# Differential attention with split scores, ScalarE taking over steps of VectorE, and new portions of the merge products (Trainium2, one core)

## The reference

```
q_d = dq.reshape(B, N, H_D, 2, DK_D)          # H_D = 4, DK_D = 64
k_d = dk.reshape(B, N, H_D, 2, DK_D)
v_d = dv.reshape(B, N, H_D, DV_D)             # DV_D = 128
if latent:
    q_d = _rope(q_d, cos_d, sin_d)
    k_all = concat([ctx[2], _rope(k_d, cos_d, sin_d)])   # 128 cached + 512
    v_all = concat([ctx[3], v_d])
p = softmax(q0 k0^T / 8) - lam * softmax(q1 k1^T / 8)
o_d = p @ v
o_d = _rms(o_d, diff_norm_g) * (1 - lam_init)
y = g_m * (o_m @ w_br_mlstm) + g_a * (o_a @ w_br_mla) + g_d * (o_d @ w_br_diff)
```

## Time and profile before

| what | value |
|---|---|
| three runs | 2631.68, 2633.82, 2633.03 us; median 2633.03 |
| the profiled execution | 2634.0 us, span 2632.2 us |
| PE busy | 2533.6 us (96%), 17328 products |
| PEld busy | 2367.1 us (90%) |
| DVE busy | 1250.5 us (48%), 1699 instructions |
| ACT busy | 750.8 us (29%), 1373 instructions |
| POOL busy | 1330.7 us (51%), 607 instructions |
| differential attention | 569 to 721 us in layer 0, 1863 to 2015 in layer 1 |
| dq/dk stage | ends at 541 us in layer 0, at 1824 in layer 1 |

### The profile page before, as it was taken

One profiled execution on the slowest core, in us unless ns is written; L12 is line 12 of the kernel. 1 busy time (PEld: TensorE's weight loads), 2 busy tenths in 40 slices (PEclk: granted clock), 3 DMA queues, 4 the chain that ended last, 5 costly groups with the idle time before them and its releaser, 6 DMA issues.

```text
span 2632.2 us, 41789 instructions
## 1 busy us (share of the span) xinstructions
PE 2533.6 (96%) x17328; PEld 2367.1 (90%) x17328; DVE 1250.5 (48%) x1699; ACT 750.8 (29%) x1373; POOL 1330.7 (51%) x607
## 2 busy tenths in 40 slices
PE   5999999999999999999989999999999999999997
PEld 3989986888899999999978899778888999999997
DVE  5443255866735423132554523659565363132235
ACT  3251355213322303021222513550334123112031
POOL 2535530453356666666654466106434666666664
PEclk8999999999999999999998999999999999999999
DMA  6202224531121222222211122342111222222221
GB/s 262 71 22 68 73 103 161 189 117 41 41 73 65 73 76 77 72 74 80 73 64 49 36 68 74 127 165 71 64 41 49 72 73 73 72 81 73 73 75 63
DMA packets 62556, 215.34 MB, mean 82 GB/s; under 512 B 6688, under 2 KB 11168, under 8 KB 62112
## 3 DMA queue, kind: packets, MB, share of 16 engines
q1 hardware_dynamic: 56448, 203.97, 22.7%
q10 hardware_dynamic: 5920, 8.70, 0.9%
HBM read 208.15 MB, written 4.49 MB: 81 GB/s over the span
## 4 chain that ended last, share of the span: by engine, by line
PE 84%; DVE 7%; issue 3%; ACT 2%; POOL 1%; DVEq 1%; DMA 1%; SPq 1%; POOLq 0%; ACTq 0%
PE big L517 21%; PE big L520 21%; PE big L521 21%; PE four L703 3%; PE big L774 3%; PE four L786 2%; PE four L599 2%; PE four L805 2%; PE big L543 1%; PE big L726 1%; PE big L546 1%; PE big L547 1%; PE four L746 1%; DVE prob_d L1651 1%; DVE prob_d L1649 1%
## 5 line engine op out<-in xcount | busy, mean ns | idle before, releaser
L481 POOL TENSOR_TENSOR w_hi<-raw,cst 128x1024 fp32r<-128x1024 f32 x288 | 552.8, 1919 | 1177.5 <-PE big L517 886.6
L517 PE MATMUL big<-act_hi,w_hi 128*128 128x320 f32 x2528 | 790.3, 313 | 6.6 <-issue 5.6
L520 PE MATMUL big<-act_lo,w_hi 128*128 128x320 f32 x2528 | 785.3, 311 | 0.0
L521 PE MATMUL big<-act_hi,w_lo 128*128 128x320 f32 x2528 | 785.1, 311 | 0.0
L484 POOL TENSOR_TENSOR w_lo<-raw,w_hi 128x1024 fp32r<-128x1024 f32 x288 | 742.7, 2579 | 41.0
L517 PEld LDWEIGHTS big<-act_hi,w_hi 128*128 128x128 f32 x2528 | 478.6, 189 | 16.0 <-issue 14.7
L520 PEld LDWEIGHTS big<-act_lo,w_hi 128*128 128x128 f32 x2528 | 478.6, 189 | 0.7
L521 PEld LDWEIGHTS big<-act_hi,w_lo 128*128 128x128 f32 x2528 | 478.3, 189 | 0.0
L517 PE MATMUL big<-u_hi,w_hi 128*128 128x320 f32 (+1 forms) x1024 | 319.0, 312 | 1.9 <-DVE u_lo L2071 1.9
L520 PE MATMUL big<-u_lo,w_hi 128*128 128x320 f32 (+1 forms) x1024 | 317.4, 310 | 0.0
L521 PE MATMUL big<-u_hi,w_lo 128*128 128x320 f32 (+1 forms) x1024 | 317.1, 310 | 0.0
(11 more groups left out here) (306 smaller groups left out, 3832.8 us busy)
## 6 DMA issues: line engine op xcount, KB each, us to landing
raw<-in_w SPq DMA_DIRECT2D x368, 512.0 KB, 3.4
first_mod<-in_first SPq DMA_DIRECT2D x16, 512.0 KB, 15.7
x<-in_x ACTq DMA_DIRECT2D x1, 2560.0 KB, 13.1
out_y<-x SPq DMA_DIRECT2D x8, 320.0 KB, 2.6
cst<-in_const ACTq DMA_DIRECT2D x1, 1664.0 KB, 7.8
small<-in_small ACTq DMA_DIRECT2D x2, 437.0 KB, 9.2
out_C<-c_new ACTq DMA_DIRECT2D x2, 258.0 KB
v_d<-in_past ACTq DMA_DIRECT2D x2, 256.0 KB, 2.9
```

The source lines that it names most:

```text
L481: nc.gpsimd.tensor_tensor(w_hi[:, to, :], raw[:, slot, :], ones[:, 0:1].to_broadcast([P, BLK]), ALU.mult)
L517: first = mm(ps, wh, ah, start=k == 0, stop=False)
L520: mm(ps, wh, al, start=False, stop=False)
L521: last = mm(ps, wl, ah, start=False, stop=k == nk - 1)
```

## The change

It has six parts. (1) The 42 portions of merge_a are cut anew: 21 pairs of slots, of each pair 5/14 in the even slot and 9/14 in the odd one. (2) q and k of the differential attention are split into rounded part and remainder: ACT makes kd_hi, qd_hi and qd_ctx_hi (`keys_hi`, `queries_hi`), DVE kd_lo and qd_lo (`keys_lo`, `queries_lo`), for head 0 ahead of the attention, for heads 1 to 3 in the middle of the head before; scores are three products each (q_hi k_hi, q_hi k_lo, q_lo k_hi). (3) In the dq/dk stage ACT makes the crossed copies of the 32-row groups and the copy of the context columns, out of the bank, and DVE keeps three operations. (4) DVE multiplies only the column of factors by neg_lam; ACT scales the second map by it (`scale_second`), and DVE adds. (5) ACT copies the outputs; turn waits for that only ahead of its fifth piece. ACT's order in a unit is new: outputs, exponential of map 0, copyT, exponential of map 1, gates, scaling, gates, parts of q and k. (6) split_y is spread: of k = 0 to 7, three at m = 5, one at m = 6 and four at m = 7, instead of six, one and one. The squares of heads move to the space of k_d and to i % 5 == 3.

```diff
-SLOTS = 2 * (5 * H_D + 1)
+SLOTS = 5 * H_D + 1
+SLOT_PARTS, SLOT_FIRST = 14, 5
-    return 4 * PAIR_PRODUCTS * slot // SLOTS
+    return 4 * PAIR_PRODUCTS * (SLOT_PARTS * (slot // 2) + SLOT_FIRST * (slot % 2)) // (SLOT_PARTS * SLOTS)
...
+        crossed = [rs, sq[:, 0, :]]
-        head_sq = [sq[:, 0, :], sq[:, 1, :], rs[:, :], prob_d[:, 0, :]]
+        head_sq = [k_d[:, 0, 0:T], k_d[:, 1, 0:T], k_d[:, 2, 0:T], prob_d[:, 0, :]]
...
+                    if t == 0:
+                        pe.wait_ge(qk_split, l * 8 + 2 * h + 2)
-                        for m, use in enumerate(uses):
-                            last = mm(ps[:, c, 0:w], q_d[r, h, q0:q1], k_d[r, h, k0 + c * w:k0 + c * w + w],
-                                      start=True, stop=True)
+                        for term, (q, kk) in enumerate(((q_hi, k_hi), (q_hi, k_lo), (q_lo, k_hi))):
+                            for m, use in enumerate(uses):
+                                r = slice(64 * m, 64 * m + 64)
+                                last = mm(ps[:, c, 0:w], q[r, :], kk[r, :], start=term == 0, stop=term == 2)
...
                 def turn(i):
-                    if i:
-                        pe.wait_ge(out_copied, l * 20 + i)
                     for c in range(1 if t == LATE else 5):
+                        if c == 4 and i:
+                            pe.wait_ge(out_copied, l * 20 + i)
...
+            def keys_hi(l, h):
+                f(kd_hi[:, h % 2, :], k_d[:, h, :], ACT.Copy).then_inc(qk_hi, 1)
+            def queries_hi(l, h):
+                f(qd_ctx_hi[:, h % 2, :], q_d[:, h, 0:CTX], ACT.Copy)
+                f(qd_hi[:, h % 2, :], q_d[:, h, CTX:T], ACT.Copy)
...
+                def scale_second(i):
+                    act.wait_ge(second_factor, l * 20 + i + 1)
+                    f(prob_d[:, c1, 0:w], prob_d[:, c1, 0:w], ACT.Copy, scale=row_sum[:, c1:c1 + 1]).then_inc(second_scaled, 1)
+                def outputs(i):
+                    act.wait_ge(o_ready, l * 60 + 40 + i + 1)
+                    f(q_d[:, h, q0:q1], out_d[i % 2], ACT.Copy).then_inc(out_copied, 1)
                 for i in range(-1, n):
+                    if i >= 1:
+                        outputs(i - 1)
                     if i + 1 < n:
-                        exps(i + 1)
+                        exps(i + 1, (0,))
+                    if i >= 0:
+                        copyT(i)
+                    if i + 1 < n:
+                        exps(i + 1, (1,))
                     if i >= 0:
                         half_gates(l, 2 * i + 2)
-                        copyT(i)
+                    if i + 1 < n:
+                        scale_second(i + 1)
                     half_gates(l, 2 * i + 3)
-                    if i > 5 and i % 5 == 1:
-                        head_square(l, (i - 6) // 5)
+                    if 0 <= i < 15 and i % 5 == 0:
+                        keys_hi(l, i // 5 + 1)
+                    if 0 <= i < 15 and i % 5 == 1:
+                        queries_hi(l, i // 5 + 1)
+                    if i > 5 and i % 5 == 3:
+                        head_square(l, (i - 8) // 5)
...
-                    f(two_parts(stage[:, m % 2, :]), halves(t), ACT.Copy, scale=DK_D ** -0.5 if m < 4 else 1.0)\
-                        .then_inc(free[b], 1)
+                    f(two_parts(stage[:, m % 2, :]), halves(t), ACT.Copy, scale=scale)
+                    for g in range(4):
+                        r, o = slice(32 * g, 32 * g + 32), slice(32 * (g ^ 1), 32 * (g ^ 1) + 32)
+                        f(two_parts(crossed[m % 2][o, :]), halves(t)[r], ACT.Copy, scale=scale)
+                    f(dst[:, 0:CTX], t[:, 0, 0:CTX], ACT.Copy, scale=scale).then_inc(free[b], 1)
...
-                    v.tensor_scalar(p1, p1, row_sum[:, c0 + 1:c0 + 2], neg_lam, ALU.mult, ALU.mult)
+                    v.tensor_scalar(row_sum[:, c0 + 1:c0 + 2], row_sum[:, c0 + 1:c0 + 2], neg_lam, None, ALU.mult)\
+                        .then_inc(second_factor, 1)
+                    dve.wait_ge(second_scaled, l * 20 + i + 1)
                     v.scalar_tensor_tensor(p0, p0, row_sum[:, c0:c0 + 1], p1, ALU.mult, ALU.add).then_inc(p_ready, 1)
...
+                    if 0 <= i < 15 and i % 5 == 1:
+                        keys_lo(l, i // 5 + 1)
+                    if 0 <= i < 15 and i % 5 == 2:
+                        queries_lo(l, i // 5 + 1)
...
-                    for g in range(4):
-                        v.tensor_tensor(t2[o, CTX:T], src[r, CTX:T], c_("sin_d", r), ALU.mult)
-                    v.tensor_copy(dst[:, 0:CTX], src[:, 0:CTX])
+                    v.tensor_tensor(t2[:, CTX:T], crossed[m % 2][:, CTX:T], c_("sin_d"), ALU.mult)
...
-                    for k in range(0, 6) if m == 5 else ([m] if m > 5 else []):
+                    for k in {5: (0, 1, 2), 6: (3,), 7: (4, 5, 6, 7)}.get(m, ()):
```

More of the change, by code:

```diff
@@ L289, in trunk @@
         tanh_d = [stage[:, 0, :], stage[:, 1, :], prob_d[:, 2, :], prob_d[:, 3, :]]
-        head_sq = [sq[:, 0, :], sq[:, 1, :], rs[:, :], prob_d[:, 0, :]]
+        head_sq = [k_d[:, 0, 0:T], k_d[:, 1, 0:T], k_d[:, 2, 0:T], prob_d[:, 0, :]]
+        kd_hi, kd_lo = at("kd_hi", [P, 2, TK], rs_at, f32r), at("kd_lo", [P, 4, TK], A0 + 10240, f32r)
+        qd_hi, qd_lo = at("qd_hi", [P, 2, LAT], A0 + 70656, f32r), at("qd_lo", [P, 4, T], A0, f32r)
+        qd_ctx_hi = at("qd_ctx_hi", [P, 2, CTX], rs_at + 6144, f32r)
         probT_d = at("probT_d", [P, 2, 5, P], A0 + 45056)
@@ L720, in scores @@
                         wait_free(pe, l, use)
+                    if t == 0:
+                        pe.wait_ge(qk_split, l * 8 + 2 * h + 2)
                     w = (k1 - k0) // (1 if t == LATE else 2)
+                    q_hi = qd_ctx_hi[:, h % 2, :] if t == LATE else qd_hi[:, h % 2, P * t:P * t + P]
+                    q_lo = qd_lo[:, h, q0:q1]
                     for c in range((k1 - k0) // w):
[L723 to L729 removed]
+                        z = slice(k0 + c * w, k0 + c * w + w)
+                        k_hi, k_lo = kd_hi[:, h % 2, z], kd_lo[:, h, z]
+                        for term, (q, kk) in enumerate(((q_hi, k_hi), (q_hi, k_lo), (q_lo, k_hi))):
+                            for m, use in enumerate(uses):
+                                ps, b, _ = buf(use)
+                                r = slice(64 * m, 64 * m + 64)
+                                last = mm(ps[:, c, 0:w], q[r, :], kk[r, :], start=term == 0, stop=term == 2)
+                                if term == 2 and c == (k1 - k0) // w - 1:
+                                    last.then_inc(ready[b], 1)
                 def turn(i):
@@ L1139, in attend_d, with exps @@
                 n = len(units)
-                def exps(i):
+                def exps(i, maps):
                     h, t = units[i]
@@ L1144, in exps @@
                         act.wait_ge(pT_ready, l * 60 + 40 + i - 1)
-                    for m in range(2):
+                    for m in maps:
                         ps, b, _ = buf(USE["da"][2 * i + m])
@@ L1624, in half_branches, with keys_lo, queries_lo @@
                     dve.drain()
+            def keys_lo(l, h):
+                dve.wait_ge(qk_hi, l * 8 + 2 * h + 1)
+                dve.wait_ge(dk_stored, l * 16 + 16)
+                v.tensor_tensor(kd_lo[:, h, :], k_d[:, h, :], kd_hi[:, h % 2, :].bitcast(f32), ALU.subtract)\
+                    .then_inc(qk_split, 1)
+            def queries_lo(l, h):
+                dve.wait_ge(qk_hi, l * 8 + 2 * h + 2)
+                v.tensor_tensor(qd_lo[:, h, 0:CTX], q_d[:, h, 0:CTX], qd_ctx_hi[:, h % 2, :].bitcast(f32), ALU.subtract)
+                v.tensor_tensor(qd_lo[:, h, CTX:T], q_d[:, h, CTX:T], qd_hi[:, h % 2, :].bitcast(f32), ALU.subtract)
+                dve.drain().then_inc(qk_split, 1)
             def attend_d(l):
@@ L2252, in _constants @@
         put("cos_" + name, np.tile(np.concatenate([c, c]), (P // dim, 1)))
-        sign = [z, -z] if name == "d" else [-z, z]
-        put("sin_" + name, np.tile(np.concatenate(sign), (P // dim, 1)))
+        put("sin_" + name, np.tile(np.concatenate([-z, z]), (P // dim, 1)))
     p, q = np.arange(P)[:, None], np.arange(P)[None, :]
```

36 lines of the change are left out of this document (21 added, 15 removed).

## The result

The changed kernel takes 2637.59 us in the median of 13 runs (2636.02 to 2641.67), the kernel before 2632.81 (2631.10 to 2634.53, 13 runs): the ratio is 1.0021, with a 95% interval of 1.0014 to 1.0028. It is slower by 4.8 us; forecast were 18.

The account below looks back on a forecast made before the run. PE was taken to bound the kernel, with 84% of the chain. Attention +13.2, rotation +4.9 and split_y 0 made +18.1 us on the profiled 2634.0, so 2651 against the median of the runs; the range was 2618 to 2674.

Parts of the forecast that it names:

- What bounds the kernel, and the excursions to DVE: Whole chain: PE holds 84%; in the attention, six excursions a layer to DVE are long when POOL splits a weight block.
- Scores as three products: Attention scores: a latent unit takes 1.08 us instead of 1.28, a context unit slightly more; -2.8 us a layer.
- Rival (c): Attention scores: weight loads of the pairs are not hidden, 1.74 us a unit, +10.5 a layer, 2672 us; chance 0.11.
- the floor of 1.28: Attention scores: by a Trainium skill rule, twelve loads of 0.107 us allow no gain, making the total 2657 us.
- The second map through ScalarE: Attention: copyT, scaling and hand-overs make each of six excursions 1.2 us longer, +7.2 us a layer.
- Rival (a): Attention: POOL does not hold the column product, so excursions come to -2.0 us a layer; about 2633 us, chance 0.22.
- Remainders of q and k: Attention: one head's three DVE operations stand on the path, +4.0 us a layer, between 0 and +8.
- Outputs: Attention: the output copy leaves DVE for ScalarE, -0.3 us in each of six excursions, -1.8 a layer.
- Portions: Attention, merge_a: the new cuts leave PE's work the same and move only cover; counted at nothing.
- Rotation of dq and dk: dq/dk stage: extra ScalarE copies cost 7.1 us in layer 0, layer 1 gains 2.25; net +4.9 us.
- split_y: Behind the gates: k = 7's remainder still sets the end of wout's first tile; 0, between -4.3 and +1.5 us a layer.
- the held column: Attention, DVE: the one-column product by neg_lam waits until POOL's instruction ends, as L1649 did; the forecast's main case, chance 0.47.

Follow-up runs that it names:

- e4: Changed kernel with the column product on one to four columns (head h uses h + 1, the added ones unread): 2649.59 us.
- e3: Changed kernel with the second map scaled by DVE again and no scaling by ScalarE: 2650.49 us, 1.0061 to the kernel before.
- e5: Changed kernel with f32 scores as before, without rounding or remainders of q and k: 2636.07 us, 1.0011 to the kernel before.
- e7: Changed kernel with the outputs copied by DVE again: 2640.07 us, 1.0027 to the kernel before.
- e6: Changed kernel with the 42 equal portions of merge_a as before: 2625.65 us, 0.9973 to the kernel before.
- e9: Changed kernel with slot 9 ended five products earlier and slot 29 three, portions else as changed: 2628.69 us, 0.9981 to the kernel before.
- e1: Changed kernel with the rotation of dq and dk as before (one ScalarE copy, seven DVE steps): 2632.38 us, 0.9999 to the kernel before.

## Why the prediction was wrong

- **What bounds the kernel, and the excursions to DVE**: the stage was right, what PE would stand for in it was not. The forecast expected about 19 us without PE in the stretch; it is 9.85 and 10.45, hardly more than before, and the largest part is merge_a's own wait for a bank.
- **Scores as three products**: right. 1.07 and 1.08 a unit against 1.08 worked out, which is 0.146 for a pair of fp32r products where a pair of f32 ones took 0.27. Rival (c), and the floor of 1.28 that the load's columns alone would set, are out: twelve products with their loads took 1.07, edge included. The Trainium skill's other rule (a load overlaps running products where the row groups differ, "TensorE: Matmul & The Clock Gate", "The mechanism") is the one that the trace agrees with.
- **The second map through ScalarE**: the step that failed first is "So I take it as held, as L1649 was". The nearest row was of four columns, and e4 shows that one column is never held and two are. Rival (a) was the case, and its -2.0 a layer for this part (+7.2 of hand-overs, -9.2 of waiting) is near the 3.1 and 2.0 of standstill that e3 gives back. (The hand-overs as listed, 0.70 + 0.70 + 0.10 - 0.61 + 0.22, make 1.11 a unit and not 1.2, so +6.7.) What a held column costs in time is not settled: e4 has it in three heads of four and is 12 us slower than the changed kernel, where the forecast priced all four at 18.4 over both layers.
- **Remainders of q and k**: right within its bounds. The split costs 2.6 and 1.5 a layer (e5), forecast +1.2.
- **Outputs**: right in sign, 0.4 and 1.7 a layer for 1.8 (e7).
- **Portions**: the second step that failed, and the dearest: "I count it at nothing, covered by the sum". They cost 7.4 and 4.8 us a layer (e6). They move no work, but they move two products of a layer ahead of the instruction that frees their bank (e9).
- **Rotation of dq and dk**: the waits were right: 4.46 for mod_row ("about 4"), 2.96 ahead of dv in layer 0 (2.4 plus clock), 3.96 for 3.5 in layer 1. The copies were priced a little low: the four 32x640 took 0.70 each, not 0.63, so they come to 3.1 and not 2.7. In time, 4.9 was forecast and 5.8 measured (e1), which the clock in another stage makes less sure than it looks.
- **split_y**: 0 forecast, 1.2 to 1.7 a layer in the trace; that is at the upper bound of +1.5. The step that failed is that k = 7's remainder alone sets the end: PE now stands 2.77 for k = 4's, which is behind the last merge step with three more to follow, and the row behind the gates did not stay unchanged.

So two large errors of opposite sign met. With equal portions the change would have been faster, 0.9973. That the direction came out as forecast is luck: the rotation's loss was foreseen, but of the attention the term that made it slower in the forecast (the held column) was not there, and the term that turned a gain into a loss on the chip (the portions) stood at nothing. Rival (a)'s 2633 is no better founded: without the portions its attention (-2.6 a layer) was too dear by 5 to 6 us a layer, and with them it is about right.

What stays open. The parts overlap: undone one at a time, portions, second map, split and outputs come to +5.4 us in layer 0 and -1.4 in layer 1, and the whole attention changed by -1.1 and -3.2. copyT ahead of the second exponential was not undone by itself. The standstills at products 108 and 264 stay with either cut, and no run was made for them; the other runs point at their causes. That at 108 waits for gates which stand behind the scaling on ScalarE, and where DVE scales (e3) it is 0.25 in both layers. That at 264 is gone in both layers without the remainders (e5), of which one stands ahead of it in the chain (the 2.31 at 643.70), but also with the outputs on DVE (e7).

## What to carry to other kernels

A change that only moves the cuts of filler work can cost more than one that adds work: for every cut, look which buffer each piece needs and behind which instruction of another engine it is freed. When an engine takes over steps on a tile, let its first copy free the bank and work on from the copy. Price a small instruction by a row of its own operation and width; here one column and two columns behave differently.

## What the runs showed of the hardware that was not expected

- A one-column DVE product is not held by POOL's split (0.21 in 50 units of two kernels, 16 of them in the middle of a POOL instruction), the same on two, three or four columns is, until POOL ends (up to 1.88, 1.40 and 2.43). A reciprocal on two columns is not (0.17).
- The granted clock makes differences that no edit asked for. In the first mixer of layer 1, which the change does not touch, the same 57 products stand at these rows of the stretches, of the kernel before and of the changed one:

```profile
1412.80:1424.07 11.27, 10.71 (x57) 10.26 (x57) 1.92 (x2) 1.44 (x2) 8.08 (x5) 0.70 0.15 47
```

```profile
1421.72:1431.69 9.97, 9.23 (x57) 8.88 (x57) 1.92 (x2) 1.44 (x2) 7.62 (x5) 0.83 0.16 54
```

The granted clock was 0.70 in the first and 0.83 in the second, and that alone is 1.3 us. Behind the next standstill 70 products take 13.21 and 11.62 us, at 0.74 and 0.85. In the attention of layer 1 it was 4.3 between the changed kernel and e1, behind the same waits. So differences of this size between two single profiles are read here only where a wait shows them too.
